# Differential attention with the values as stationary operand in column halves, its head norm on transposed data, and six gate matmuls ahead of each unit's scores

## What is computed

```python
def diff_attention(q, k, v, lam_params, norm_g, lam_init):
    b, s, h, _, dq = q.shape
    ...
        logits = jnp.einsum('bqhrd,bshrd->bhrqs', qb, k).astype(jnp.float32) * (dq ** -0.5)
        p = jax.nn.softmax(jnp.where(visible, logits, NEG_INF), axis=-1)
        a = (p[:, :, 0] - lam * p[:, :, 1]).astype(v.dtype)
        return jnp.einsum('bhqs,bshd->bqhd', a, v)
    ...
    return head_rmsnorm(out, norm_g) * (1.0 - lam_init)
```

## Time and profile before

| | us |
|---|---|
| median of three runs (1865.0 to 1865.82) | 1865.38 |
| the profiled execution | 1862.33 |
| its span in the profile | 1860.5 |
| TensorE busy | 1734.3 (93% of the span) |
| VectorE busy | 1454.7 (78%) |
| ScalarE busy | 941.5 (51%) |
| branch D in `attend`, from its first scores to those of the first C pair | 396 to 658 |
| branch C, to about | 823 |
| branch A, to about | 967 |

### The profile page before, as it was taken

The page is one execution under the profiler, slowest core; times in us unless marked ns, Lnnn a source line. Parts: engine busy times, 40 slices in busy tenths (PEclk is TensorE's granted clock), DMA queues, the critical chain, the costliest instruction groups (busy, mean ns, idle before and its releaser), DMA issues. The chain is left out here.

```text
span 1860.5 us, 24019 instructions
## 1 busy us (share of the span) xinstructions
PE 1734.3 (93%) x8706; PEld 1311.2 (70%) x8706; DVE 1454.7 (78%) x2094; ACT 941.5 (51%) x1207; POOL 151.2 (8%) x129
## 2 busy tenths in 40 slices
PE   7999999999999999999999989759999999999980
PEld 7768887777777777777767767637777777777750
DVE  5587869989788878666539855669999999999956
ACT  6543121133344455545665510137877877777752
POOL 1100000000000000000000000002122122122003
PEclk9999999999999999999999989769999999999995
DMA  5202222112434312423216810379999999999937
GB/s 198 69 20 71 91 68 69 57 63 69 184 116 128 111 54 63 142 63 113 69 68 245 318 41 34 146 284 369 390 397 402 396 398 401 396 400 400 402 119 289
DMA packets 75920, 358.76 MB, mean 193 GB/s; under 512 B 8636, under 2 KB 11228, under 8 KB 49340
## 3 DMA queue, kind: packets, MB, share of 16 engines
q1 hardware_dynamic: 66364, 324.08, 46.5%
q0 software_dynamic: 5888, 20.97, 3.4%
q10 hardware_dynamic: 3584, 12.58, 1.7%
HBM read 301.63 MB, written 55.98 MB: 192 GB/s over the span
## 5 line engine op out<-in xcount | busy, mean ns | idle before, releaser
L2362 DVE TENSOR_TENSOR wa_lo<-wa,w_hi 128x2048 fp32r<-128x2048 f32 x127 | 287.6, 2286 | 15.5 <-ACT w_hi L2275 14.1
L2275 ACT ACTIVATE w_hi<-wa 128x2048 fp32r<-128x2048 f32 x127 | 242.8, 1915 | 63.0 <-PE psum L2220 36.4
L1470 PE MATMUL psum<-h_hi,w_hi 128*128 128x512 f32 x512 | 211.9, 414 | 4.2 <-DVE w_lo L153 2.1
L1470 PE MATMUL psum<-h_hi,w_lo 128*128 128x512 f32 x512 | 204.6, 400 | 0.0
L1470 PE MATMUL psum<-h_lo,w_hi 128*128 128x512 f32 x512 | 202.0, 395 | 0.0
L167 DVE MAX8 top<-sel 128x8 f32<-128x384 f32 (+5 forms) x192 | 171.3, 892 | 4.8
L2369 DVE TENSOR_TENSOR wb_lo<-wd,w_hi 128x2048 fp32r<-128x2048 f32 x64 | 143.9, 2288 | 34.6 <-ACT w_hi L2284 34.6
L165 DVE MATCH_REPLACE8 sel<-top,sel 128x384 f32<-128x384 f32 (+5 forms) x192 | 168.1, 875 | 0.0
L2204 PE MATMUL psum<-w_hi,xT_hi 128*96 128x512 f32 x512 | 164.6, 402 | 1.9 <-DVE xT_lo L2377 1.9
L2204 PE MATMUL psum<-w_hi,xT_lo 128*96 128x512 f32 x512 | 161.2, 396 | 0.0
L2204 PE MATMUL psum<-wa_lo,xT_hi 128*96 128x512 f32 x512 | 161.0, 396 | 0.0
(11 more groups left out here) (372 smaller groups left out, 3376.7 us busy)
## 6 DMA issues: line engine op xcount, KB each, us to landing
wa<-expert_up SPq DMA_DIRECT2D x128, 1024.0 KB, 11.2
wd<-expert_down SPq DMA_DIRECT2D x64, 1024.0 KB, 11.3
w<-w_gate SPq DMA_DIRECT2D x32, 512.0 KB, 4.1
gate_pre<-gate_out SPq DMA_DIRECT2D x64, 256.0 KB, 2.5
gate<-gate_pre SPq DMA_DIRECT2D x32, 512.0 KB, 6.2
ys<-yo ACTq DMA_DIRECT2D x32, 384.0 KB, 6.9
w<-w_T SPq DMA_DIRECT2D x18, 512.0 KB, 3.7
ys<-zeros SPq DMA_DIRECT2D x7, 1152.0 KB, 5.9
```

Source lines behind the costliest of these rows:

```text
L1470: ins = nc.tensor.matmul(psum[:, 7, :], w[:, k, :], x[:, k, half * 512:(half + 1) * 512], start=(n == 0), stop=(n == BURST - 1))
L2275: nc.scalar.activation(hi_a(j, q).rearrange("p c m n -> p (c m n)"), wa[j][q][:, :, :, :].rearrange("p c m n -> p (c m n)"), ACT.Copy).the ...
L2362: nc.vector.tensor_tensor(wa_lo[j][q][:, :, :, :].rearrange("p c m n -> p (c m n)"), wa[j][q][:, :, :, :].rearrange("p c m n -> p (c m n)" ...
```

## The change

Five things change, all in `attend` but for a table of gains:

- D is divided by its first sum before the difference: VectorE takes the reciprocal right after `maxima(u)` (`inverse(u)`), ScalarE multiplies the first exponential by it (`scale(u)`) after the second exponential and ahead of the gate copy, and `differ(u)` waits for that (`scaled`).
- D's weights meet the values as those of C and A do: two heads together, values stationary in halves of the array's columns. The products of a pair of units stand in the slot of the second head. The output is transposed, and `norm` is a plain copy, one unit later.
- The head norm of D works on the transposed output: the squares (2048 columns) are summed over each head by four matmuls of 512 columns with a matrix of ones (`halves`) after pair NB + 8, ScalarE takes the root of every element of these, and at NB + 12 VectorE takes 128 x 2048 reciprocals and multiplies twice 1024 columns at NB + 13. The reduction, the 32 roots and the 16 transposes go.
- The transposes of branch B's result, which stood after unit 10, stand after unit 11.
- TensorE runs 6 of the 24 gate matmuls ahead of the scores in each slot of D, 6 behind them, and the groups of a unit are transposed together.

```diff
 def attend(nc, a, s):
...
-    Y_AT = {"D": 10, "C": 16}
+    Y_AT = {"D": 11, "C": 8}
...
+                    if what == "D":
+                        act.wait_ge(aneg_ready, 1)
+                        nc.scalar.activation(sq[:, c, t0 * P:(t0 + 4) * P], src, ACT.Sqrt, bias=eps[:, 0:1],
+                                             scale=1.0 / HD).then_inc(pt_copied, 1)
+                        at[0] += 1
+                        return
...
             def scale(u):
                 wd = keys(*units[u][0:2])[1] * P
                 buf = pbuf[bufs(u)[0]][:, 0:wd]
-                act.wait_ge(inv_ready, u - NB + 1)
+                act.wait_ge(inv_ready, u + 1)
...
                 if u < NB:
                     act.wait_ge(stats_ready, n_exp[u] + 2)
                     diff_exp(1)
+                    scale(u)
                 if u and u - 1 in burst_after:
                     gate_store(burst_after[u - 1])
...
-            norm_at = {NH * n + (4 if n < NT else 6): n for n in range(NU // NH)}
+            norm_at = {NH * n + (5 if n < NT - 1 else 4 if n < NT else 6): n for n in range(NU // NH)}
...
                 link(nc.vector.reciprocal(stat[:, v % 4, 4:5], sums[:, b % 2, h, 1:2]))
-                link(nc.vector.scalar_tensor_tensor(out=stat[:, v % 4, 5:6], in0=stat[:, v % 4, 4:5],
-                                                    scalar=sums[:, b % 2, h, 0:1], in1=lam[:, 4:5],
-                                                    op0=ALU.mult, op1=ALU.mult))
+                link(nc.vector.tensor_tensor(stat[:, v % 4, 5:6], stat[:, v % 4, 4:5], lam[:, 4:5], ALU.mult))
+                dve.wait_ge(scaled, v + 1)
...
                 if u == NB + 2:
-                    link(nc.vector.tensor_tensor(sq[:, :, :], heads, heads, ALU.mult))
...
+                    nc.vector.tensor_tensor(sq[:, :, :], y[:, :, :], y[:, :, :], ALU.mult).then_inc(squared, 1)
+                elif u == NB + 12:
+                    dve.wait_ge(pt_copied, copied_by["D"])
+                    link(nc.vector.reciprocal(sq[:, :, :], sq[:, :, :]))
+                elif u == NB + 13:
+                    for c in range(2):
+                        ins = nc.vector.scalar_tensor_tensor(out=y[:, c, :], in0=y[:, c, :], scalar=gain_T[:, c:c + 1],
+                                                             in1=sq[:, c, :], op0=ALU.mult, op1=ALU.mult)
+                    ins.then_inc(y_ready, 1)
...
             for u in range(NB):
                 if u:
                     differ(u - 1)
                 maxima(u)
+                inverse(u)
...
+                    if what == "D":
+                        pe.wait_ge(squared, 1)
+                        pe.wait_ge(halves_ready, 1)
+                        nc.tensor.matmul(psum[:, 4 + i % 2, :], halves[:, :], sq[:, c, t0 * P:(t0 + 4) * P],
+                                         start=True, stop=True).then_inc(pt_ready, 1)
+                        continue
...
-                if g0 == 0:
-                    if what + 1 < NB:
-                        score(what + 1, 1)
-                    else:
-                        score(NB, 2)
-                    if what:
-                        gate(gates_before(what), 2 * quarter)
-                    pe.wait_ge(diff_ready, what + 1)
-                turn(i)
-                if last:
-                    gate(gates_before(what) + 2 * quarter, quarter)
-                weigh_waiting()
-                waiting.append(i)
-                if last:
-                    gate(gates_before(what) + 3 * quarter, quarter)
-                    weigh_waiting()
+                if g0:
+                    continue
+                quarter, n = BURST // 4, 1 if last else 2
+                if what:
+                    gate(gates_before(what), quarter)
+                if what + 1 < NB:
+                    score(what + 1, 1)
+                else:
+                    score(NB, 2)
+                if what:
+                    gate(gates_before(what) + quarter, quarter)
+                pe.wait_ge(diff_ready, what + 1)
+                for g in range(n):
+                    if i + g >= 2:
+                        pe.wait_ge(pt_copied, i + g - 1)
+                    turn(i + g)
+                for g in range(2):
+                    gate(gates_before(what) + (2 + g) * quarter, quarter)
+                    if h % 2 and g < n:
+                        m = weighed[0]
+                        weigh(i - n + g, i + g, m + g, m + n + g, 2 if n == 1 else 1 + 2 * g)
```

More of the change, by code:

```diff
@@ L991, in attend @@
     pt = [sb(f"pt{i}", [P, 512], 155.25 + 2 * i) for i in range(4)]
-    sq = sb("sq", [P, NT * NH, HD], 163.25)
+    sq = sb("sq", [P, 2, SEQ], 163.25)
+    halves = sb("halves", [P, P], 203.5)
     bias = sb("bias", [P, NH, BAND], 112.25)
@@ L1162, in _ @@
             pool.memset(mask01[0:CH, 3 * P - CH:3 * P], NEG).then_inc(mask_ready, 1)
+            pool.wait_ge(mask_ready, 1)
+            link(pool.memset(halves[:, :], 0.0))
+            link(pool.memset(halves[0:HD, 0:HD], 1.0))
+            pool.memset(halves[HD:P, HD:P], 1.0).then_inc(halves_ready, 1)
+            pool.wait_ge(halves_ready, 1)
             pool.memset(zeros[:, :], 0.0).then_inc(zeros_ready, 1)
@@ L1224, in _ @@
                         act.wait_ge(pt_ready, ready_after[prev])
-                    if h == 0 and u // NH >= 2:
-                        act.wait_ge(out_normed, u // NH - 1)
                     act.wait_ge(stats_ready, n_exp[u] + 1)
@@ L1281, in norm @@
                 dve.wait_ge(pv_done, pv_after[n * NH + NH - 1])
[L1282 to L1292 removed]
+                nc.vector.tensor_copy(out_of[kind][:, :, b * P:(b + 1) * P],
+                                      psum[:, 6, 0:2 * P].rearrange("p (c n) -> p c n", c=2)).then_inc(out_normed, 1)
+            norm_at = {NH * n + (5 if n < NT - 1 else 4 if n < NT else 6): n for n in range(NU // NH)}
             def differ(v):
@@ L1430, in _, with weigh @@
             values = {"D": s.v2, "C": s.v1, "A": s.v2}
-            def weigh(i, m):
-                u, g0, ng, last = groups[i]
+            def weigh(i0, i1, m0, m1, freed):
+                u, g0, ng, last = groups[i0]
                 kind, b, h = units[u]
                 k0, nk = keys(kind, b)
-                n = u // NH
-                if kind != "D":
-                    pe.wait_ge(pt_copied, i + 2)
-                    if h == 0 and g0 == 0:
-                        pe.wait_ge(out_normed, n)
-                    for j in range(ng):
-                        for r in range(2):
-                            ins = nc.tensor.matmul(psum[HD * r:HD * r + HD, 6, h // 2 * P:(h // 2 + 1) * P],
-                                                   values[kind][:, k0 + g0 + j, (h + r) * HD:(h + r + 1) * HD],
-                                                   pt[(m + r) % 4][:, j * P:(j + 1) * P],
-                                                   start=(g0 + j == 0), stop=(g0 + j == nk - 1))
-                    ins.then_inc(pv_done, 2)
-                    return
-                pe.wait_ge(pt_copied, i + 1)
-                if h == 0 and g0 == 0 and n:
-                    pe.wait_ge(out_normed, n)
-                for j in range(ng):
-                    ins = nc.tensor.matmul(psum[:, 6, h * HD:(h + 1) * HD], pt[m % 4][:, j * P:(j + 1) * P],
-                                           values[kind][:, k0 + g0 + j, h * HD:(h + 1) * HD],
-                                           start=(g0 + j == 0), stop=(g0 + j == nk - 1))
-                ins.then_inc(pv_done, 1)
+                pe.wait_ge(pt_copied, i1 + 1)
+                if h == 0 and g0 == 0 and u:
+                    pe.wait_ge(out_normed, u // NH)
+                for j in range(ng):
+                    for r, m in enumerate((m0, m1)):
+                        ins = nc.tensor.matmul(psum[HD * r:HD * r + HD, 6, h // 2 * P:(h // 2 + 1) * P],
+                                               values[kind][:, k0 + g0 + j, (h + r) * HD:(h + r + 1) * HD],
+                                               pt[m % 4][:, j * P:(j + 1) * P],
+                                               start=(g0 + j == 0), stop=(g0 + j == nk - 1))
+                ins.then_inc(pv_done, freed)
             def gate(first, count):
@@ L1482, in weigh_waiting @@
                     i = waiting.pop()
-                    weigh(i, weighed[0])
-                    weighed[0] += 1 if units[groups[i][0]][0] == "D" else 2
+                    weigh(i, i + 1, weighed[0], weighed[0] + 1, 2)
+                    weighed[0] += 2
             def turn(i):
@@ L1502, in pair @@
                     pe.wait_ge(pt_copied, i + r - 1)
-                    pe.wait_ge(scaled, u + r - NB + 1)
+                    pe.wait_ge(scaled, u + r + 1)
                     turn(i + r)
```

60 lines of the change are left out of this document (16 added, 44 removed).

## The result

The changed kernel takes **1898.13 us** (median of 4 runs, 1896.7 to 1902.05), the kernel before 1865.19 (4 runs beside them, 1863.07 to 1865.82): ratio 1.0183, 95% interval 1.0171 to 1.0196. The forecast was 1896, range 1881 to 1907. The profiled execution took 1897.66 us, with a span of 1895.9.

The account below looks back on a forecast made before the run. TensorE's stream was taken as the bound. D +18.6 and C +12.3 gave +30.9 us, turning the profiled 1862.33 into 1893.2; as that execution lay 3.05 below the median, the forecast was 1896 us, range 1881 to 1907.

Parts of the forecast that it names:

- D, products: D's products with the values: two heads side by side gain 6.4 us, switches taking two thirds of what packing halves.
- D, the gate bank: D: gate bursts touching on one PSUM bank cost 0.95 us at 23 boundaries, +21.9 us; shorter stalls in blocks 4 to 7, +1.1.
- D, ScalarE: D: scalings ahead of the gate copy delay it, +1.7 us in blocks 6 and 7 and +1.3 at unit 11.
- The -1.0 for waits that go: D: of TensorE's present waits for the gate copy, 2.3 us at most, 1.0 us disappears.
- C, the sums: C: four float32 matmuls for the norm's sums, 3.7 us with switches, replace 16 transposes: +1.3 us (0 to 3).
- C, the piece on VectorE: C: reciprocal of 12.4 us plus multiplications delays masking, so TensorE stalls 8.3 us at scores; +9.0 us with the second head's.
- The rivals at 2.3 and 22 us: C's reciprocal lasts 2.3 us, or 22 us, instead of 12.4: 1885 us (chance 0.08), or 1905 us (no separate chance).
- C, the clock: C: TensorE, idle for 8.3 us, loses its clock and then runs at 0.50: +2.0 us (0 to 4).
- covered waits: Rival for D and C: every new wait finds cover, nothing waits, 1862 us; chance 0.03.
- no change: Rival for the whole kernel: the waits merge with others, time within 4 us of 1865; chance 0.02.
- the streaming and the longer reciprocal: C: reciprocal streams, no stall or lost clock, 1885 us, chance 0.08; at 22 us the stall grows, 1905 us.
- ScalarE as D's bound: Rival for D: exponentials meet copies late from block 4, 16 slots each 0.6 us longer, +8, 1904 us; chance 0.08.

Follow-up runs that it names:

- e1: The changed kernel with all 12 gate matmuls of D behind the scores, none ahead: 1871.29 us, ratio 1.0041.
- e5: e1 with D's products issued head after head instead of alternating between the two heads: 1876.69 us, ratio 1.007.
- e6: e1 with both product groups of a pair of units in one burst right before the next scores: 1864.99 us, ratio 0.9998.
- e8: e6 with D's norm moved from C to A, the reciprocal in eight pieces in A's first units: 1857.48 us, ratio 0.9964.
- e9: e8 with the eight reciprocal pieces in every second unit of A from its 17th, multiplications at A's last unit: 1853.4 us, ratio 0.9934.
- e7: e1 with the reciprocal over 128x1024 instead of 128x2048, so half of D's norm isn't computed: 1864.48 us, ratio 0.9998.
- e10: The changed kernel with every gate burst in D begun six matmuls earlier, so its last six stand ahead of the next scores: 1872.4 us, ratio 1.0034.
- e4: The changed kernel with three gate matmuls ahead of D's scores and nine behind, instead of six and six: 1897.78 us, ratio 1.0179.

## Why the prediction was right

**D, products (forecast -6.4).** e1 against before gives -7.4 for all that is not the order. e5 and e6 show what it is made of: the halves run together (5.9 us), and each passage costs (5.3 us for fewer of them, where the same prices give 6). The forecast's term was for the products alone; what scaling, regrouped transposes and fewer waits add to the 7.4 was not measured apart. By the forecast's own numbers the switches take 8.4 of the 14.8 us that halving would give, rather over a half than two thirds; the sum of 6.4 doesn't use it.

**D, the gate bank (forecast +21.9 and +1.1).** The count of boundaries was right. Between bursts that follow directly there are 1.08 us after even units, and 1.17 to 1.18 after the seven odd units of blocks 0 to 3. With the slower gap behind it (0.33 or 0.32), and less two paces, that is 0.95 and 1.03 per boundary, so 12 x 0.95 + 7 x 1.03 = 18.6 us for the 19 without ScalarE's part, where 18.1 was forecast. The odd units of blocks 4 to 7 have gaps of 0.68, 0.68, 0.47 and 0.47 from the last product to the first gate matmul, where a free passage is 0.20: 1.5 us instead of 1.1.

**D, ScalarE (forecast +1.7 and +1.3).** In block 7 the two boundaries are 1.74 instead of 1.08, in block 6 1.32 and 1.31: 2 x 0.66 + 2 x 0.24 = 1.8 us. The gap behind unit 11 is 2.81 us from the last transpose to the first gate matmul. Against it the forecast had set a shift of 1.2 us in the kernel before, and that is there, in the scores that follow B's transposes (the second row is the next unit's scores):

```profile
475.88 2.17 PE L1423 MATMUL psum<-k,q 32*128 32x512 f32 x4 [0.20 <-ACT k L1197]
...
484.64 1.13 PE L1423 MATMUL psum<-k,q 32*128 32x512 f32 x4
```

So this place costs 2.8 - 1.0 = 1.8 us more than before, where 1.3 was forecast. e1 has such a shift too, 1.4 us in slot 12. The order's terms come to 18.6 + 1.5 + 4 x 0.95 + 1.8 + 2.8 = 28.5 us, less these 1.4 is 27.1; the changed kernel's D against e1's is 28.8, less the 1.4 of the moved cut 27.4. The -1.0 for waits that go wasn't seen: e1 has no fewer of them than the kernel before. D was forecast at 18.6, and came to 21.4 as cut and 20.0 for the same work.

**C, the sums (+1.3).** This term was too small. With the rest of the norm gone from C, e8 and e9 keep +1.8, but that is a net. In e9 the slots NB + 8 to NB + 18 take 3.0 us more than before the change: the sums themselves are 3.7, as estimated (+4.7 and -1.0 in slots NB + 8 and NB + 10, one product having moved from the second to the first), but in slots NB + 16 and NB + 18, where the transposes stood, only 1.4 came back and not 2.4, with a new wait of 0.7 for the norm's copy there, and slot NB + 12 is 0.6 longer, a wait for the gate copy. The forecast had neither wait. Slots 31 and NB take 1.1 less together, since TensorE's gap at the start of C falls from 2.32 to 0.73 us; the forecast let it stay.

**C, the piece on VectorE (+9.0).** The reciprocal took 12.95 us against an estimated 12.4, 4% more, the multiplications 2.5, and the stall is 8.26 us start to start against 8.3. Slot NB + 12 takes 17.20 us, 7.9 more than e9's 9.27, where the piece is not in C. e7 shows that the stall follows the piece one to one. The rivals at 2.3 and 22 us fell.
**C, the clock (+2.0).** After 7.87 us idle TensorE had 0.50 for 5.4 us, as forecast, and the slot that begins there took 12.09 us instead of 9.09. But that the clock is what cost this isn't shown, and e7 speaks against it: at the full clock its slots NB + 14 and NB + 16 take 11.06 + 11.76 = 22.8 us, the changed kernel's 12.09 + 10.72 = 22.8. Without the piece, in e9, they take 9.19 + 11.36 = 20.6. So these two slots lose 2.3 us behind the piece, at either clock: e1 shows the same sum at half the clock with waits of 0.6 and 0.6 for the gate copy and the norm's copy, e7 at the full one with 1.30 and 1.12, so what TensorE gains in pace it spends waiting for these two. **The clock fell as forecast and the size came near, but the runs don't bear out that the one made the other; that is luck.** So is the total of C: its piece and clock came to 7.9 + 2.3 = 10.2 us for 11.0, and its sums to 3.0 for 1.3.

**Of the rivals**, covered waits, no change, the streaming and the longer reciprocal and ScalarE as D's bound are out by the rows above. ScalarE's row sets the gap at four boundaries, not at sixteen slots. Sum forecast 30.9, difference of the medians 32.9. What stays open is why the boundaries after odd units are 0.1 us longer than those after even ones. The copy is no slower there: after unit 1 it starts 0.43 us behind the last gate matmul's start and takes 0.60, and the next burst begins 0.14 behind its end, 0.06 after unit 4. A burst after an odd unit is the first on a new weight tile and waits for `w_low_done` besides, which may be the cause; no run was made for it.

## What to carry to other kernels

A matmul burst that accumulates in the only bank of its kind needs something else on TensorE between its last matmul and the next burst's first, at least as long as the reader's reply (here 1.08 us). Where pieces of a burst are moved, move the point at which it begins too (e10). An element-wise operation that costs nanoseconds per element belongs where its engine waits, in pieces shorter than that wait, and not in front of what frees a bank; where such a place isn't in the same stage, the next one may have it (e9). A part of a change that gains should be tried without the others: here the new form of D's products was worth 7.4 us in D, hidden under an order that cost 27 and a norm that made C 12 longer. And a stage's length says what an edit does only if the stage holds the same work and the same clock in both executions: slot by slot, e4's gain was 1.9 us where the stage showed 0.9.

## What the runs showed of the hardware that I had not expected

- VectorE's reciprocal costs 6.4 and 6.3 ns per element of a partition at 1024 and 2048 elements (6.55 and 12.95 us), and 6.8 in pieces of 256 (1.75 us).
- Two runs of half-width matmuls into different column halves overlap even when one stands wholly behind the other: 16 records take 1.51 us so, 1.03 alternating, where 1.76 was expected without overlap (16 x 0.11).
- TensorE behind 7.87 us of idleness ran 5.4 us at half clock. Behind e7's idle time of 1.47 us it kept the full one, but behind 1.66 us of waiting in slot NB e7 had half the clock, where the changed kernel, after a wait of the same length, had none of it.
- The same program can be granted half the clock at one place in one execution and not in another: about 3.5 us in slot 12 of e8, none in e9, worth 1.6 us. Seven of the twelve profiled executions have one such stretch or more in D or C besides the one behind the long stall.
- Half a clock need not cost time: behind the stall in C, e7 at 1.00 and the changed kernel at 0.50 take the same 22.8 us for two slots.
- Three gate matmuls ahead of the scores cost as much as six, to 0.35 us of the medians.
